# Modulation rows of a four-layer transformer by way of DRAM as eight pieces of 512 bytes, and another order of layer 1's mixer

## What is computed

```python
def first_block(x, c, positions, ada_w, ada_b, ...):
    c_act = jax.nn.silu(c)
    for l in range(2):
        mod = c_act @ ada_w[l] + ada_b[l]
        shift_m, scale_m, gate_m, shift_f, scale_f, gate_f = split(mod, 6)
        h = rms_norm(x, g_pre_mix[l]) * (1.0 + scale_m) + shift_m
        q, k, v, u = split(h @ w_in[l] + b_in[l])
        attn_out = sliding_window_attention_with_sinks(rotary(q), rotary(k), v, sinks[l])
        pool_out = causal_pool_mixer(u, pool_w[l], pool_scale[l])
        mix = concatenate([attn_out, pool_out]) @ w_out[l]
        x = x + gate_m * rms_norm(mix, g_post_mix[l])
        h = rms_norm(x, g_pre_ffn[l]) * (1.0 + scale_f) + shift_f
        f = (silu(h @ w_gate[l]) * (h @ w_up[l])) @ w_down[l]
        x = x + gate_f * rms_norm(f, g_post_ffn[l])
    return x
```

## Time and profile before

| | us |
|---|---|
| median of three runs | 1191.18 (1190.67 to 1191.89) |
| the profiled execution, as timed | 1190.44 |
| its span, first to last instruction | 1188.6 |
| PE busy in it | 1145.2 (96%) |
| DVE busy | 809.1 (68%) |
| ACT busy | 634.3 (53%) |
| POOL busy | 25.6 (2%) |

### The profile page before, as it was taken

One profiled execution on the slowest core, in us unless ns is written; L12 is line 12 of the kernel. 1 busy time (PEld: TensorE's weight loads), 2 busy tenths in 40 slices (PEclk: granted clock), 3 DMA queues, 4 the chain that ended last, 5 costly groups with the idle time before them and its releaser, 6 DMA issues.

```text
span 1188.6 us, 19635 instructions
## 1 busy us (share of the span) xinstructions
PE 1145.2 (96%) x7899; PEld 1024.6 (86%) x7899; DVE 809.1 (68%) x1255; ACT 634.3 (53%) x1114; POOL 25.6 (2%) x61
## 2 busy tenths in 40 slices
PE   5989999999999999999999999999999999999997
PEld 3556999998878999999888799999989889999996
DVE  5798966797986755655676667666566757765663
ACT  3067443456557644435655766555556577555543
POOL 2200000000000000000000000000000000000000
PEclk9999999999999999999999999999999999999999
DMA  9994999997543766585343355544544434555530
GB/s 376 410 420 193 333 324 298 320 377 277 190 154 117 282 236 227 206 265 174 126 178 107 142 206 183 207 178 178 180 141 156 144 106 178 212 179 190 198 106 36
DMA packets 37305, 252.97 MB, mean 213 GB/s; under 512 B 4416, under 2 KB 4704, under 8 KB 8928
## 3 DMA queue, kind: packets, MB, share of 16 engines
q1 hardware_dynamic: 34992, 244.47, 57.2%
q0 software_dynamic: 2080, 7.25, 1.6%
q10 hardware_dynamic: 144, 0.00, 0.0%
HBM read 250.64 MB, written 1.06 MB: 212 GB/s over the span
## 4 chain that ended last, share of the span: by engine, by line
PE 84%; DVE 8%; DMA 3%; ACT 3%; issue 1%; SPq 0%; DVEq 0%; ACTq 0%
PE bank L490 25%; PE bank L492 25%; PE bank L491 25%; PE bank L497 3%; DMA raw_w<-weights 3%; DVE raw_w L1586 2%; PE bank L585 2%; PE bank L539 2%; DVE lo_w L1576 2%; PE bank L628 1%; ACT gtok L1138 1%; PE bank L928 1%; DVE prob L1732 1%; DVE tok L1795 0%; DVE smax L1735 0%
## 5 line engine op out<-in xcount | busy, mean ns | idle before, releaser
L1576 DVE TENSOR_TENSOR lo_w<-raw_w,hi_w 128x1024 fp32r<-128x1024 f32 (+3 forms) x346 | 408.9, 1209 | 124.3 <-ACT hi_w L1133 123.8
L1133 ACT ACTIVATE hi_w<-raw_w 128x1024 fp32r<-128x1024 f32 (+3 forms) x346 | 350.5, 1041 | 151.3 <-DMA raw_w<-weights 88.2
L490 PE MATMUL bank<-in_hi,lo_w 128*128 128x256 f32 x1408 | 395.8, 281 | 0.0
L491 PE MATMUL bank<-in_lo,hi_w 128*128 128x256 f32 x1408 | 392.9, 279 | 0.0
L492 PE MATMUL bank<-in_hi,hi_w 128*128 128x256 f32 x1408 | 392.9, 279 | 0.0
L490 PEld LDWEIGHTS bank<-in_hi,lo_w 128*128 128x128 f32 x1408 | 264.3, 188 | 2.5 <-issue 0.8
L491 PEld LDWEIGHTS bank<-in_lo,hi_w 128*128 128x128 f32 x1408 | 263.6, 187 | 1.9 <-issue 0.5
L492 PEld LDWEIGHTS bank<-in_hi,hi_w 128*128 128x128 f32 x1408 | 264.7, 188 | 0.0
L490 PE MATMUL bank<-hi_w,in_lo 128*128 128x256 f32 (+2 forms) x464 | 143.9, 310 | 8.6 <-DVE in_lo L1687 2.4
L492 PE MATMUL bank<-hi_w,in_hi 128*128 128x256 f32 (+2 forms) x464 | 141.0, 304 | 0.0
L491 PE MATMUL bank<-lo_w,in_hi 128*128 128x256 f32 (+2 forms) x464 | 140.8, 303 | 0.0
(11 more groups left out here) (216 smaller groups left out, 1080.0 us busy)
## 6 DMA issues: line engine op xcount, KB each, us to landing
raw_w<-weights SPq DMA_DIRECT2D x215, 1024.0 KB, 5.7
ink<-ink_w SPq DMA_DIRECT2D x8, 640.0 KB, 13.2
rows<-norm_rows POOLq DMA_DIRECT2D x5, 512.0 KB, 4.9
ink<-whole_w SPq DMA_DIRECT2D x2, 1024.0 KB, 23.1
early_out<-whole_w SPq DMA_DIRECT2D x2, 1024.0 KB, 13.9
rows<-mod_rows POOLq DMA_DIRECT2D x4, 512.0 KB, 9.2
raw_w<-weights SPq DMA_DIRECT2D x2, 832.0 KB, 4.4
const<-const_table SPq DMA_DIRECT2D x1, 1538.0 KB, 8.0
```

The lines of the kernel that those rows point to most:

```text
L490: nc.tensor.matmul(o, st[1], mv[0], start=start, stop=False, **kw)
L491: nc.tensor.matmul(o, st[0], mv[1], start=False, stop=False, **kw)
L1133: nc.scalar.activation(hi_w[:, m % NSPLIT, cut], raw_view(unit)[:, cut], ACT.Identity).then_inc(*sig("hi_w", unit, i))
L1576: nc.vector.tensor_tensor(lo_w[:, m % NSPLIT, cut], raw_view(unit)[:, cut], hi_w[:, m % NSPLIT, cut].bitcast(F32), ALU.subtract).then_inc( ...
```

## The change

- Four rows that went to DRAM element by element, and the three spread rows of layer 1, all go by one way now: PE transposes the column [128 x 8] into a bank (`turn_column`), ACT copies the 8 x 128 numbers to `pieces` (two buffers, `piece`), POOL writes them to DRAM as eight runs of 512 bytes (`row_out`) and loads them back on all partitions (`row_back`). `TURN_AFTER` says after which feed-forward product a column is turned. A piece's buffer is written again only when the transfer out of it, two rows earlier, has landed.
- (1, gate, 0) goes back into slot 0 once the last `gained` of layer 0 has used the old gate; (1, scale, 1) is turned in the input projection; (1, shift, 1) is turned between the two attention products.
- On ACT in layer 1, `pooled_in`, both `pool_hi` and the second half of wo 3 come ahead of the exponentials of scores 4 and 5. On DVE the division of score 4 comes behind `pool_lo` and the second half of wo 3, and the split of wo 1 ahead of `attn_lo`.
- On PE, probability tile 5 is turned ahead of wo 2's products for T = 1, and wo 3's products for T = 1 come after the attention products.

```diff
--- before.py
+++ after.py
@@ -120,6 +120,11 @@
     (L, kind, w) for L in range(2) for w in range(2) for kind in ("shift", "scale", "gate"))}
 
 
+TURN_AFTER = {("gu", 0, 8): (0, "gate", 1), ("gu", 0, 12): (1, "shift", 0), ("gu", 0, 16): (1, "scale", 0), ("gu", 0, 20): (1, "gate", 0),
+              ("gu", 1, 19): (1, "gate", 1)}
+TURNED = [*list(TURN_AFTER.values())[:4], (1, "scale", 1), (1, "shift", 1), (1, "gate", 1)]
+
+
 ADA_AFTER = {}
 _order = [(0, 20 + _i) for _i in range(4)] + [(1, _i) for _i in range(12)] + [(1, 16 + _i) for _i in range(4)]
 _f = [("gu", 0, _i) for _i in range(2, 22)]
@@ -343,6 +348,8 @@
         gatew = sb("gatew", [16, 2, P])
         poolw = sb("poolw", [P, 2, 4, P])
 
+        pieces = sb("pieces", [P, 2, P])
+
         ssq = sb("ssq", [P, 2, 2])
         sbias = sb("sbias", [P, 2, 1])
         tok_rstd = sb("tok_rstd", [P, 2, 2])
@@ -629,6 +636,13 @@
                                                 start=True, stop=True)
                     last.then_inc(*sig(*job))
 
+            def turn_column(L, kind, w):
+
+                pe.wait_ge(*due("modcol", L, kind, w))
+                job = ("column", L, kind, w)
+                b = take(job)
+                nc.tensor.transpose(b[0:KT, 0:P], modcol[:, ROWS[(L, kind, w)], :], k("ident")).then_inc(*sig(*job))
+
             def front(name, N, L, units):
 
                 def run(T, between=None):
@@ -706,8 +720,9 @@
                     banks(4, 5, 6, 7, 2, 3)
                     scores_late()
                 else:
-                    banks(4, 5, 6, 7, 0, 1, 2, 3, 4, 5, 6, 7, 2, 3)
+                    banks(4, 5, 3, 6, 7, 0, 1, 2, 3, 4, 5, 6, 7, 2, 3)
                     both_halves(lambda T: ("in", 1, T, 1), ("in", 1, 2))
+                    turn_column(1, "scale", 1)
                     turn_qk(0, 0)
                     turn_qk(1, 0)
                     for T in range(2):
@@ -772,9 +787,8 @@
                     into_y(1, 0, ("wo", 1, 2), 0, first=True)
                     into_y(1, 0, ("wo", 1, 3), 0)
                     turn_prob(4)
+                    turn_prob(5)
                     into_y(1, 0, ("wo", 1, 2), 1, first=True)
-                    turn_prob(5)
-                    into_y(1, 0, ("wo", 1, 3), 1)
 
                 def attention(jp):
                     job = ("attn", L, jp)
@@ -793,12 +807,12 @@
 
                 if L == 0:
                     spread_row(L, "gate", 0)
-                for jp in range(2):
-                    attention(jp)
+                attention(0)
                 if L == 1:
-                    spread_row(L, "gate", 0)
-                    spread_row(L, "scale", 1)
-                    spread_row(L, "shift", 1)
+                    turn_column(1, "shift", 1)
+                attention(1)
+                if L == 1:
+                    into_y(1, 0, ("wo", 1, 3), 1)
 
             def attention_mixed(L):
 
@@ -952,6 +966,8 @@
                         product(("gu", L, i), ("gu", L, i), both)
                         if i == 2:
                             turn_back(1)
+                        if (kind, L, i) in TURN_AFTER:
+                            turn_column(*TURN_AFTER[(kind, L, i)])
                     else:
                         for T in range(2):
                             into_y(L, 1, ("wd", L, i), T, first=(i == 0))
@@ -1047,8 +1063,8 @@
             def row_out(L, kind, w):
 
                 n = ROWS[(L, kind, w)]
-                pool.wait_ge(*due("modcol", L, kind, w))
-                pool.dma_start(mod_rows[n, :].rearrange("(t p) -> p t", p=P), modcol[:, n, :], allow_slow_non_contiguous=True).then_inc(
+                pool.wait_ge(*due("piece", L, kind, w))
+                pool.dma_start(mod_rows[n, :].rearrange("(t p) -> t p", p=P), pieces[0:KT, TURNED.index((L, kind, w)) % 2, :]).then_inc(
                     *sig("row_out", n, by=16))
 
             def row_back(L, kind, w):
@@ -1090,7 +1106,13 @@
             mod_row(0, "gate", 1)
             mod_row(1, "shift", 0)
             mod_row(1, "scale", 0)
+            row_out(1, "gate", 0)
+            pool.wait_ge(*due("gained", "y", 0, 1, 1, 1))
+            row_back(1, "gate", 0)
             sinks_in(1)
+            row_out(1, "scale", 1)
+            row_back(1, "scale", 1)
+            mod_row(1, "shift", 1)
             pool.wait_ge(*due("normed", ("ffn", 1), 1, 1))
             mod_row(1, "gate", 1)
             plain_row(("mix", 2))
@@ -1202,6 +1224,13 @@
                 slot = ("gate", "scale", "shift").index(kind)
                 for c in range(2):
                     copy(("spread", L, kind, w, c), rows[:, slot, cols(c)], ps(("spread", L, kind, w, c))[:, :], "row", L, kind, w, c)
+
+            def piece(L, kind, w):
+
+                n = TURNED.index((L, kind, w))
+                if n >= 2:
+                    sc.wait_ge(*due("row_out", ROWS[TURNED[n - 2]]))
+                copy(("column", L, kind, w), pieces[0:KT, n % 2, :], ps(("column", L, kind, w))[0:KT, 0:P], "piece", L, kind, w)
 
             def by_tile(bank):
                 return bank[:, :].rearrange("p (t s) -> p t s", s=P)
@@ -1307,6 +1336,7 @@
                     probT_in(3)
                 else:
                     prepare(("in", 1, 4))
+                    piece(1, "scale", 1)
                     for T in range(2):
                         qk_in(T, 0)
                     prepare(("wo", 1, 2))
@@ -1318,13 +1348,13 @@
                     probT_in(1)
                     prepare(("wo", 1, 3), (0,))
                     probT_in(2)
-                    exps(4)
                     pooled_in()
-                    exps(5)
-                    probT_in(3)
                     pool_hi(0)
                     pool_hi(1)
                     prepare(("wo", 1, 3), (1,))
+                    exps(4)
+                    exps(5)
+                    probT_in(3)
                 if L == 0:
                     probT_in(4)
                     probT_in(5)
@@ -1340,9 +1370,8 @@
                     for jp in range(2):
                         sc.wait_ge(*due("attn", 1, jp))
                         nc.scalar.activation(in_hi[:, 2 * jp:2 * jp + 2, :], ps(("attn", 1, jp))[:, :], ACT.Identity).then_inc(*sig("attn_hi", 1, jp))
-                    row_in(1, "gate", 0)
-                    row_in(L, "scale", 1)
-                    row_in(L, "shift", 1)
+                        if jp == 0:
+                            piece(1, "shift", 1)
                     prepare(("gu", 1, 0))
                     prepare(("gu", 1, 1))
 
@@ -1509,6 +1538,8 @@
                                 conv0(early)
                             silu_of(early)
                             round_hidden(early)
+                    if (kind, L, f - 1) in TURN_AFTER:
+                        piece(*TURN_AFTER[(kind, L, f - 1)])
                     if kind == "gu":
                         if L >= 2:
                             conv0(f)
@@ -1616,10 +1647,7 @@
 
                 if L >= 2:
                     return
-                if w == 0:
-                    ve.wait_ge(*due("row", L, "gate", 0, c))
-                else:
-                    ve.wait_ge(*due("row0", L, "gate", 1))
+                ve.wait_ge(*(due("row", 0, "gate", 0, c) if (L, w) == (0, 0) else due("row0", L, "gate", w)))
                 job = ("y", L, w, T, c)
                 ve.wait_ge(*due("squared", L, w, T, c))
                 if T == 1:
@@ -1644,7 +1672,7 @@
 
                 for c in range(2):
                     if T == 0:
-                        ve.wait_ge(*(due("row1", N[1], "scale", 0) if N[0] == "mix" else due("row", N[1], "scale", 1, c)))
+                        ve.wait_ge(*(due("row", 0, "scale", 1, c) if N == ("ffn", 0) else due("row1", N[1], "scale", 0 if N[0] == "mix" else 1)))
                     else:
                         ve.wait_ge(*due("normed", N, 0, c))
                     ve.wait_ge(*due("x", *before(N), T, c))
@@ -1662,10 +1690,7 @@
                         ins = nc.vector.tensor_scalar(dst, x[:, T, cols(c)], r, None, ALU.mult)
                     elif modulated(N):
                         ve.wait_ge(*due("scaled", N, T, c))
-                        if N[0] == "ffn":
-                            ve.wait_ge(*due("row", N[1], "shift", 1, c))
-                        else:
-                            ve.wait_ge(*due("row2", N[1], "shift", 0))
+                        ve.wait_ge(*(due("row", 0, "shift", 1, c) if N == ("ffn", 0) else due("row2", N[1], "shift", 0 if N[0] == "mix" else 1)))
                         ins = nc.vector.scalar_tensor_tensor(dst, scaled[:, cols(c)], r, rows[:, 2, cols(c)], ALU.mult, ALU.add)
                     else:
                         row, _ = norm_row(N)
@@ -1895,15 +1920,15 @@
                     shares(3)
                     scored(5)
                     lo(("wo", 1, 3), (0,))
-                    shares(4)
                     pool_lo(0)
                     pool_lo(1)
                     lo(("wo", 1, 3), (1,))
```

(4 more changed lines are left out.)

## The result

The changed kernel takes 1183.24 us (median of four runs, 1183.14 to 1183.39), the kernel before 1190.93 (four runs, 1190.37 to 1191.89). The ratio is 0.9938, 95% interval 0.9921 to 0.9954: 7.7 us faster, where 8.55 were forecast (1182.6). Run again beside other kernels (e5) it was 1182.48 (six runs, 1181.67 to 1184.23) against 1190.02, ratio 0.9940 (0.9926 to 0.9954).

What follows compares the result with a forecast made beforehand. TensorE (PE), busy for 96% of the span, was taken to bound the kernel. The terms - 5.4 - 2.3 - 1.6 + 0.75 = - 8.55 us took 1191.18 to 1182.6 us as timed, range 1180.8 to 1187.0.

Steps and rivals of the forecast that it cites:

- Part 1: Layer 1's mixer: three spread rows leave PE's chain, 5.57 us, for one column turn at 0.15; gain 5.4 us.
- The step on the cover: Layer 1's mixer: wo 3's T = 1 products, moved behind the attention, cover the attention tiles' residual parts; uncovered, 1.4 us.
- The split of wo 1 at nothing: Layer 1's mixer, DVE: moving this split ahead of attn_lo costs and saves nothing.
- Part 2: Layer 1's mixer: pooled work sooner on ACT and DVE starts PE's first output product 2.3 us sooner.
- rival (d): Layer 1's mixer: prob 4 and 5 come late by what the pooled work won; 1186.5 us, chance 0.06.
- Part 3: Layer 1's mixer: with less PE idle time, the clock no longer halves for eight products; gain 1.6 us.
- Rival (a): Layer 1's mixer: the clock drops all the same, there or a little later; 1184.2 us, chance 0.15.
- Part 4: Feed-forwards of layers 0 and 1: five column turns on full PE cost 0.75 us; ACT's small copies are hidden.
- Part 5: DRAM transfers: four element-wise ones go, worth 0 to 0.5 us, taken as 0; new round trips arrive in time.
- The slack of the shift row: Layer 1's mixer: the row is back at 365.7, the first normed needs it at 368.8; 3.1 us.
- Rival (b): Shift row or last gate row late by less than the gain; 1183 to 1188.5 us, chance 0.13.
- rival (c): Layer 1's first norm: the DRAM way replaces the spreads on the path, 14.8 late, slower at 1197.4 us; chance 0.02.

Runs made afterwards that it cites:

- e3: Changed kernel with the feed-forwards' five rows sent to DRAM element by element again, without turn or copy: 1186.88 us against 1190.75 for the kernel before.
- e9: The kernel of e3 run again, unchanged: 1183.75 us against 1190.09 for the kernel before.
- e1: Changed kernel with layer 1's three spread rows put back on PE: 1187.02 us against 1190.75 for the kernel before.
- e6: Changed kernel with the (1, shift, 1) column turned ahead of both attention products: 1182.52 us, the changed kernel beside it 1182.48.
- e7: Changed kernel with wo 3's products for T = 1 back ahead of the attention products: 1182.05 us, ratio 0.9941 to the kernel before.
- e10: Changed kernel with the split of wo 1 back behind attn_lo on DVE: 1183.50 us, ratio 0.9946 to the kernel before.
- e2: Changed kernel with ACT's and DVE's old order around the pooled features: 1184.92 us against 1190.75 for the kernel before.
- e11: Kernel before with only the pooled work sooner on ACT and DVE: 1186.86 us against 1190.09 for the kernel before.
- e4: Kernel before with seven small filler products on PE ahead of the first output product: 1190.99 us against 1190.75 for the kernel before.
- e8: Changed kernel with the shift row sent to DRAM and back twice: 1189.22 us against 1190.02 for the kernel before.

## Why the prediction was right

**What bounds the kernel.** Right. PE's waits in layer 0's feed-forward are now

```profile
PE bank L497 <- DVE hid_lo L2084: 0.6, 2, 0.4
```

against 0.5: in the profiles the slow transfers had cost PE no wait. Whether they lengthened other executions is left open by e3 and e9.

**Part 1, the spreads.** The mechanism was right, its size 0.6 us too large: 4.8 (e1) instead of 5.4. The step that failed is the price of the turn between the attention products, taken at 0.15 from four turns in a row. It is 3.66 - 3.04 = 0.62, since it cuts a group in two whose products overlap: each of the 48 holds an operand of 128 x 64, half of the array, and they follow each other every 3.04 / 48 = 0.063 us, where full 128 x 128 transposes need 0.44 / 4 = 0.11. Moved ahead of the group (e6), the same turn gives back 0.52. That explains 0.47 of the 0.6; no run separates the rest. The step on the cover failed as well, harmlessly: "without that cover it would cost 1.4" counted the last attention tiles as what wo 0 waits for, and wo 0 doesn't read them (e7). The split of wo 1 at nothing was right (e10).

**Part 2, the order.** 2.3 forecast, 2.28 in the profile, 2.24 and 2.28 in e2 and e11. DVE's 0.64 us from `pool_lo` to the product carried over: 343.61 to 344.24. That `prob` 4 and 5 would be in time was right; rival (d) is out.

**Part 3, the clock.** 1.6 forecast, 1.53 to 1.56 in the stretches (e2, e4, e11). Rival (a), the fall comes all the same, was wrong for the place it was about. But the forecast took the fall of one profile for that of every execution. As a gain of the whole time the 1.6 us isn't shown (e4, e11), and this is the one term of the sum that stays unproven there: the clock also falls in the first 70 us, in one run and not in another, and that is as large as what was won here.

**Part 4, the turns.** 0.15 each was taken. The timeline of PE at the turn of (1, shift, 0):

```profile
213.14 0.28 PE L499 MATMUL bank<-in_hi,hi_w 128*128 128x256 f32 x1
213.26 0.27 PE L644 MATMUL bank<-const,modcol 128*8 128x128 f32 x1
213.28 0.37 PE L497 MATMUL bank<-in_hi,lo_w 128*128 128x256 f32 x1
213.48 0.28 PE L498 MATMUL bank<-in_lo,hi_w 128*128 128x256 f32 x1
```

From 213.14 to 213.48 three products start; elsewhere in this row of products two starts take 0.24 us. So the turn costs 0.34 - 0.24 = 0.10, and five cost 0.5 rather than 0.75. That layer 0's feed-forward gets longer by it is not shown: from its first `silu` it took 168.2 us before and 168.6 after, but 168.9 and 169.6 in e11 and e4, which have no turn in it. The copy of a piece, 8 x 128, takes 0.25 at 356.02 above, and only POOL's transfer waits for it.

**Part 5, the transfers.** The slack of the shift row was put at 3.1 us and is 2.9, which is luck in part. From the end of ACT's copy (356.27) to the landing (368.0) it took 11.7 us, not 10.7: the way out 4.9 instead of 3.7 us to land, the return 6.2 instead of 7, and 0.6 us for the issues, which the sum left out. And `normed` came 0.9 later than summed (370.90 less 1.20 is 369.7, not 368.8), 0.5 of it from the turn between the attention products. Rival (b) didn't happen, but it was near, and e8 shows that its price was set too low: past the slack, more than one for one. The 16.3 us of rival (c) is a load of `c_norm_rows` behind three others, not a row's return; the longest of those in the kernel before took 9.7. The Trainium skill, DMA: Bandwidth & Descriptors, section Anatomy of one DMA — SWDGE (gpsimd) path, gives 2.0 us for a transfer of almost no bytes. The gate row at 542.84, with its return issued 1.9 us later, agrees; the shift row at 356.58 took 5.2 while weights landed, and the measurement decides. The same page's section Issuing engines are not separate DMA queues says that the DMAs of all issuing engines run on the same 16 DMA engines and interleave. The shift row agrees: POOL issued it, and its 5.2 us fell in a stretch in which SP's weights moved at 365 GB/s.

**The sum.** The two stretches were put at 5.4 + 2.3 + 1.6 = 9.3 us and gave 8.64; less 0.5 for the turns instead of 0.75 that is 8.1, where 8.55 were forecast: the two misses cancel in part. The whole time gave 7.7 and 7.5, intervals 5.5 to 9.4 and 5.5 to 8.8. The 0.5 us between can be chance, or part 3 in the executions that never had the fall.

## What to carry to other kernels

When a matrix engine is full, count the instructions that a relayout costs it before counting bytes: 48 records for three rows became three turns. The round trip through DRAM hides as long as the due time is worked out for the loaded queue and not for the quiet one. Put a short odd instruction between full products rather than inside a group of half-array products: here it cost 0.1 us at one place and 0.6 at the other. Judge an edit of 1 us by the stretch it is in: the whole time of this kernel moves by more than that through the clock alone. But a stretch of one profile is one execution; what it gains is a gain of the kernel only when the whole times agree.

## What the runs showed that I had not expected

- A turn of 8 columns costs PE 0.10 us between full products and 0.62 between two groups of half-array products.
- Eight pieces of 512 bytes take 1.9 us until the return can be issued when the DMA engines move 37 GB/s, and 2.7 to 5.2 beside weights: 2.7 at 299 GB/s, 5.1 at 250, 5.2 at 365 in the changed kernel. So the load alone doesn't set it.
- A wait of PE of 6 us at the norm (e8) brings half clock from 376 to about 383 us, 1.7 us on top of the wait.
- The clock falls in the first 70 us in nine of 13 profiles, for 3 to 4 us each time, at a place that changes with the run; in the two profiles of e3's kernel it falls twice.
